# A two-layer hybrid decoder step on eight cores: the order of the token mixing, the first norm's sums, the last group of the output projection and the last block

## What is computed

```python
def trunk_layer(h, ...):                       # two layers, then a final rmsnorm
    z = rmsnorm(h, norm_mix) @ w_in            # 2048 -> 4352: 34 tiles of 128 columns
    # u_a 512, glu_a 768, glu_b 768, sc_b 768, sc_c 768, sc_h 768
    y_a = pool_mixer(u_a)                      # causal means over 2, 4, 8, 16 rows, 128x128 map
    g = glu_a * sigmoid(glu_b)
    cb = layernorm(causal_dwconv31(g) + b)     # width 31
    y_b = silu(cb) @ conf_pw + conf_pw_b
    y_c = sc_b * causal_dwconv3(sc_c * sc_h)   # width 3
    h = h + concat([y_a, y_b, y_c]) @ w_out
    up = rmsnorm(h, norm_ffn) @ w_up
    upc = causal_dwconv3(up)
    h = h + (silu(upc[..., :D_FF]) * upc[..., D_FF:]) @ w_down
    gate = sigmoid(rmsnorm(h, norm_ple) @ ple_gate)
    return h + (p_i @ ple_proj) * gate, <last rows of each convolution's input>
```

## Time and profile before

| | |
|---|---|
| median of 3 runs | 3181.56 us (3180.45 to 3588.96) |
| profiled execution | 3180.19 us |
| its longest span (core 1) | 3178.6 us |
| spans of the other cores | 3168.2 to 3176.3 us |
| TensorE busy, core 1 | 3053.5 us (96%) |
| VectorE | 1717.0 us (54%) |
| ScalarE | 875.0 us (28%) |
| GpSimd | 503.0 us (16%) |

### The profile page before, as it was taken

One profiled execution on the slowest core, in us unless ns is written; L12 is line 12 of the kernel. 1 busy time (PEld: TensorE's weight loads), 2 busy tenths in 40 slices (PEclk: granted clock), 3 DMA queues, 4 the chain that ended last, 5 costly groups with the idle time before them and its releaser, 6 DMA issues.

```text
span 3178.6 us, 58865 instructions; the slowest of 8 cores (3168.2 to 3178.6 us)
## 1 busy us (share of the span) xinstructions
PE 3053.5 (96%) x21015; PEld 1976.6 (62%) x21015; DVE 1717.0 (54%) x3475; ACT 875.0 (28%) x1743; POOL 503.0 (16%) x732
## 2 busy tenths in 40 slices
PE   4899999999999999999999799999999999999995
PEld 1455666666666666666666466666666666666674
DVE  2455425655555555656544633375555555565665
ACT  2214012312131213315551321232212121331565
POOL 4100032010000000015320001311010000001532
PEclk8778999999999999999999999999999999999998
DMA  6543473463544344444346335546444445344444
GB/s 165 113 89 53 70 118 60 80 99 67 85 71 81 70 76 72 81 75 74 61 84 133 58 66 103 78 81 105 74 79 79 79 70 87 69 85 76 74 68 108
DMA packets 126205, 263.28 MB, mean 83 GB/s; under 512 B 36320, under 2 KB 68576, under 8 KB 125920
## 3 DMA queue, kind: packets, MB, share of 16 engines
q0 software_dynamic: 74112, 213.48, 41.0%
q1 hardware_dynamic: 43744, 35.20, 4.5%
q10 hardware_dynamic: 8064, 10.84, 1.4%
HBM read 449.11 MB, written 15.97 MB: 146 GB/s over the span
## 4 chain that ended last, share of the span: by engine, by line
PE 89%; DVE 4%; DMA 2%; issue 1%; ACT 1%; POOL 1%; SPq 1%; ACTq 0%; DVEq 0%; POOLq 0%
PE ps L130 89%; DVE xa L130 2%; DVE U L130 2%; DMA h<-xT 1%; POOL U L130 1%; SPq L130 1%; ACT U L130 1%; DMA U<-hf 0%; DVE h L130 0%; ACT L130 0%; DVE xb L130 0%; ACT rstd L130 0%; ACTq L130 0%; DMA xa<-U 0%; DMA U<-hc 0%
## 5 line engine op out<-in xcount | busy, mean ns | idle before, releaser
L130 PE MATMUL ps<-xa,wb 128*128 128x364 bf16 (+7 forms) x9504 | 1483.4, 319 | 41.5 <-DVE xa L130 19.0
L130 PE MATMUL ps<-xb,wb 128*128 128x366 bf16 (+8 forms) x9760 | 1437.9, 309 | 12.5 <-DVE U L130 9.9
L130 PEld LDWEIGHTS ps<-xa,wb 128*128 128x128 bf16 x9504 | 935.3, 99 | 579.4 <-issue 64.0
L130 PEld LDWEIGHTS ps<-xb,wb 128*128 128x128 bf16 x9760 | 944.3, 98 | 493.8 <-issue 19.0
L130 DVE SCALAR_TENSOR_TENSOR U<-ps,cstt,U 128x348 f32<-128x348 f32 (+3 forms) x1056 | 607.2, 577 | 429.1 <-ACT U L130 372.7
L130 ACT ACTIVATE U<-ps,cstt 128x364 f32<-128x364 f32 (+2 forms) x528 | 290.3, 553 | 1165.6 <-PE ps L130 1105.4
L130 DVE TENSOR_TENSOR h<-ps,h 128x364 f32<-128x364 f32 (+4 forms) x672 | 348.4, 523 | 413.6 <-PE ps L130 412.7
L130 POOL TENSOR_TENSOR U<-U 128x364 f32<-128x364 f32 (+6 forms) x311 | 261.3, 845 | 354.1 <-ACT U L130 347.3
L130 ACT ACTIVATE U<-h 128x344 bf16<-128x344 f32 (+11 forms) x352 | 169.1, 483 | 448.5 <-DVE h L130 394.5
L130 ACT ACTIVATE U<-U 128x364 f32<-128x364 f32 (+4 forms) x418 | 200.5, 480 | 254.5 <-DVE U L130 193.2
L130 POOL DMA_DIRECT2D wb<-w_up x176 | 93.7, 532 | 1051.5 <-PE ps L130 1051.5
(11 more groups left out here) (64 smaller groups left out, 829.5 us busy)
## 6 DMA issues: line engine op xcount, KB each, us to landing
wb<-w_up POOLq DMA_DIRECT2D x176, 512.0 KB, 6.4
wb<-w_in POOLq DMA_DIRECT2D x68, 512.0 KB, 7.0
wb<-w_down POOLq DMA_DIRECT2D x64, 448.0 KB, 6.6
wb<-w_out POOLq DMA_DIRECT2D x32, 512.0 KB, 9.9
wb<-w_down POOLq DMA_DIRECT2D x32, 512.0 KB, 5.4
wb<-ple_gate POOLq DMA_DIRECT2D x32, 512.0 KB, 5.1
h<-xT SPq DMA_DIRECT2D x8, 728.0 KB, 33.3
h<-xT SPq DMA_DIRECT2D x4, 752.0 KB, 14.9
```

The costliest lines, as they stand in the source:

```text
L130: ins = getattr(e, name)(*a, **kw)
```

## The change

1. First norm: ScalarE's 16 squares of a block stay in SBUF (`sq0`), and 16 products by ones sum them; GpSimd adds nothing. `first_norm(b + 1)` now follows `first_rstd(b)`, since all blocks share `sq0`. The weight loads 4 and 5 wait for block 2's input instead of block 1's, and the constants are loaded behind the whole input.
2. Mixing: `sc_triple(0)` stands ahead of `conf_conv(5)`; mean, variance and output of the layer norm are cut into blocks and put behind the blocks of triples 1 and 2; triple 3 follows, then `conf_out`, then the pooling with triples 4 and 5 between its parts. A triple multiplies both h and c by the root (three operations instead of two with its square). `phys` says where in C_t each concatenated tile lies; tile 10 lies in U_t. w_out reads the pooling tiles last, in the first tile as single products. The sample history of the convolution has one buffer instead of two.
3. The last group of w_out has six tiles (`WTAIL`), and `tick` issues the ones product three jobs later.
4. End: three blocks, all pieces on VectorE.

```diff
-                while pend and pend[0][0] <= st["tick"] - 2:
+                while pend and pend[0][0] <= st["tick"] - 3:
...
             def first_norm(b):
                 lo, hi = b0(b)
                 for k in range(KC):
-                    stats0.add(k, b)
+                    S.op("act", (lambda e: e.activation(out=sq0[k][0][:, 0:hi - lo], in_=h1(k, lo, hi), func=AF.Square)), reads=of(hB[k], b), writes=[sq0[k][1]])
...
+            def first_rstd(b):
+                lo, hi = b0(b)
+                slot = bank()
+                mm(slot, hi - lo, KC, (lambda k: ones_t[:]), (lambda k: sq0[k][0][:, 0:hi - lo]), [onesB] + [o for _, o in sq0])
+                rstd_from(slot, of(rsB, b), lo, hi)
...
-                        if first and b < 2:
-                            first_norm(b + 1)
                         slots = [[xjob(wbuf, wv[:, 0], lo, hi, b) for wbuf, wv in ws[j]] for j in js]
                         if b == 2:
                             ring.done(2 * len(js))
                         if first:
-                            go0.pop(0)()
+                            first_rstd(b)
+                            if b < 2:
+                                first_norm(b + 1)
...
-                        S.op("dve", (lambda e: e.tensor_tensor(out=V[:, 0:n + 2], in0=ps_t[:, sc_, 0:n + 2], in1=hv[:, 0:n + 2], op=ALU.mult)),
-                             reads=[psB[sc_], hvB], writes=[VB])
+                        S.op("dve", (lambda e: e.tensor_tensor(out=V[:, 0:n + 2], in0=ps_t[:, sc_, 0:n + 2], in1=rstd_t[:, lo - 2:hi], op=ALU.mult)), reads=[psB[sc_]] + rs, writes=[VB])
+                        S.op("dve", (lambda e: e.tensor_tensor(out=V[:, 0:n + 2], in0=V[:, 0:n + 2], in1=hv_[:, 0:n + 2], op=ALU.mult)), reads=[hvB], writes=[VB])
...
+                        if b in mids:
+                            mids[b]()
...
-                pool_proj(3)
-                conf_dgen(5)
+                sc_triple(0, {0: lambda: conf_dgen(5)})
                 conf_conv(5)
...
+                sc_triple(1, {b: (lambda b=b: ln_mean(b)) for b in range(3)})
+
+                def var_out(b):
+                    if b == 0:
+                        ln_var()
+                    ln_out(b)
+                sc_triple(2, {b: (lambda b=b: var_out(b)) for b in range(3)})
+                sc_triple(3)
+                conf_out()
...
+                pool_proj(3)
                 pool_sums(3)
                 pool_hist(1)
+                sc_triple(4)
                 pool_proj(2)
-                ln_mean()
                 pool_sums(2)
                 pool_hist(0)
+                pool_mm(3)
                 pool_proj(1)
                 pool_sums(1)
                 pool_proj(0)
                 pool_sums(0)
...
-                sc_triple(0)
-                for g in (3, 2, 1, 0):
+                sc_triple(5)
+                for g in (2, 1, 0):
                     pool_mm(g)
-                conf_out()
-                for j in range(1, 6):
-                    sc_triple(j)
...
-                for ms in [[m] for m in range(KC - TAIL)] + [list(range(KC - TAIL, KC))]:
+                for ms in [[m] for m in range(KC - WTAIL)] + [list(range(KC - WTAIL, KC))]:
...
-                eb = Blocks(z0 + 32, (CUT1, CUT2, CUT3, W)) if last else fb
+                eb = fb
...
-                            eng = "pool" if b == eb.n - 1 and k == 12 else "dve"
```

More of the change, by code:

```diff
@@ L371, in go @@
                         slot = bank()
[L372 to L375, removed]
+                        S.op("pe", (lambda e: e.matmul(ps_t[:, slot, 0:n], lhsT=onesf_t[:], rhs=sa[:, 0:n], start=True, stop=False)), reads=[onesB, saB], writes=[psB[slot]])
+                        mm(slot, n, 1, (lambda k: ones_t[:]), (lambda k: sq[:, 0:n]), [onesB, sqb], first=False)
                         rstd_from(slot, of(rsB, b, self.blk.n), lo, hi)
                         self.after(b)
[L378 to L381, removed]
+                    pend.append((st["tick"], go))
             def rstd_from(slot, rb, lo, hi):
@@ L568, in ln_sum, with ln_mean @@
                     return slot, lo, hi, hi - lo
[L570 to L576, removed]
+                def ln_mean(b):
+                    slot, lo, hi, n = ln_sum(b)
+                    for j in JO:
+                        S.op("dve", (lambda e: e.scalar_tensor_tensor(out=CB_v[:, j, lo:hi], in0=ps_t[:, slot, 0:n], scalar=-1.0 / 768, in1=CB_v[:, j, lo:hi],
+                                                                      op0=ALU.mult, op1=ALU.add)), reads=[psB[slot]], writes=[CBB[j][b]])
+                        S.op("act", (lambda e: e.activation(out=sil_v[:, j, lo:hi], in_=CB_v[:, j, lo:hi], func=AF.Square)), reads=[CBB[j][b]], writes=[silB[j][b]])
                 def ln_var():
@@ L686, in after_first @@
                     conf_hist(0)
-                    conf_hist(1)
+                    shs, shsB = late["shs"]
+                    s4 = shs.rearrange("p (j k b) -> p j k b", j=6, k=2)
+                    S.dma("sp", (lambda e: e.dma_start(out=shs.rearrange("p (j c) -> p j c", j=6), in_=hs_in[l])), "s_hs", writes=[shsB])
                     S.dma("pool", (lambda e, l=l: e.dma_start(out=wpl_v, in_=w_pool[l * 512:(l + 1) * 512, :].rearrange("(g c) d -> c g d", c=128))),
@@ L737, in program @@
-                S.op("dve", (lambda e: e.tensor_tensor(out=shc[0].rearrange("p (j b) -> p j b", j=6), in0=s4[:, :, 0, :], in1=s4[:, :, 1, :], op=ALU.add)), reads=[shs[1]], writes=[shc[1]])
-                sc_triple(0)
-                for g in (3, 2, 1, 0):
+                sc_triple(5)
+                for g in (2, 1, 0):
                     pool_mm(g)
-                conf_out()
-                for j in range(1, 6):
-                    sc_triple(j)
                 S.dma("sp", (lambda e: e.dma_start(out=ns_out[l], in_=ns_t[:])), "s_ns", reads=[nsB])
-                cats = catB
+                order = list(range(4, KC)) + list(range(4))
@@ new lines, in wjob, with fn @@
+                def wjob(wbuf, wv, lo, hi, b, split):
+                    slot = bank()
+                    groups = [order[0:11]] + [[k] for k in order[11:]] if split else [order]
+                    for ks in groups:
+                        def fn(e):
+                            for k in ks:
+                                e.matmul(ps_t[:, slot, 0:hi - lo], lhsT=wv[:, k, :], rhs=catv(k, lo, hi), start=(k == order[0]), stop=(k == order[-1]))
+                        S.op("pe", fn, reads=[wbuf] + [catB[k][b] for k in ks], writes=[psB[slot]])
+                    tick()
+                    return slot
```

134 lines of the change are left out of this document (67 added, 67 removed).

## The result

The changed kernel takes 3073.51, 3076.33 and 3076.73 us where the kernel before took 3180.45 and 3181.56: a ratio of 0.9668 (95% interval 0.964 to 0.9696), 106 us less. The forecast was 3103 with a range of 3064 to 3140; what came is rival (a), 3073.

A forecast was written before the change was run, and what follows sets the result against it. TensorE, busy 96% of the span, bounds the kernel, so only its waits and clock losses can be won: -26 - 7 - 5 - 27 - 12 = -77 gives 3103 us with the low clock, -107 or 3073 without; range 3064 to 3140.

The forecast's parts named there:

- rival (a): Whole kernel: no core at clock 0.80, waits go and nothing replaces them; 3073 us, 3064 to 3088; chance 0.28.
- first norm: Start: without GpSimd adds, the second weight pair's products begin at 74 instead of 100.43 us; -26 us.
- layer 0's mixing: Layer 0, convolutions to projection: waits go but the 0.80 clock stays as long; -7 us, or -37 without it.
- layer 1's mixing: Layer 1, same new order: waits for replicas and VectorE go; -27 us, bounds -28 and -14.
- group and tick: Projection's last group of six tiles: VectorE gets more time for norm products; -5 us, bounds 0 and -7.
- plain end: After block 1's last tile: 38 us instead of 50.3, last output issued after about 31; -12, bounds -16 and -4.
- bound of -29: Start: the first norm's gain without the dip to 1.2 GHz while TensorE follows the scalings.
- the -4 of the plain end: End of the kernel: the smallest gain allowed for the plain end, whose term was -12 us.
- VectorE's cover: Mixing: VectorE's triple and layer norm work, 6.8 us a block, fits beside TensorE's at 80 to 95%.
- rival (b): Mixing: VectorE takes TensorE's place, half the waits return; 3120 to 3138 us; 0.21 with (d) and longer low clock.
- Rival (c): Whole kernel slower: low clock holds while TensorE has no long pause; 3450 us if held to 1640; chance 0.06.
- Rival (d): Start shortens less, block 2's input or next weight tiles late; ten of 26 us lost, 3113; within rival (b)'s 0.21.

The follow-up runs named there:

- the one execution that bears on it: Changed kernel with weight tiles three and four released earlier and the last block's squares 13 and 14 summed by TensorE; 3092.33 us, cores 4 and 5 at mean clock 0.986.
- both candidates: Changed kernel with weight tiles three and four released by the input's second quarter, last block's squares 13 and 14 summed by TensorE; 3065.4 to 3066.86 us, ratio 0.9647.

## Why the prediction was right and wrong

| step | forecast | runs |
|---|---|---|
| first norm | -26 | 26 to 28 |
| layer 0's mixing | -7 (-37 without low clock) | 31.6 |
| layer 1's mixing | -27 | 28.8 |
| group and tick | -5 | 2.5, unresolved |
| plain end | -12 | 16 |
| sum | -77 (-107) | 105 to 107; 101 to 105 with 56 or 57 for both mixings, of 106 |

The step that failed is the -7 for layer 0's mixing in the sum: -37 less 30 us of a clock at 0.80, with which the forecast takes it that a core of the changed kernel stands at 0.80 as long again. None did in the three executions. All their mean clocks are between 0.991 and 0.995, the profiled one has 1.00 from 120 to 300 us on every core, and the mixing gave 31.6 us.
The condition itself, "If the clock stands at 0.80 as long again, the gain is -7", is not what the runs speak against: the one execution that bears on it, 3092.33 beside 3065.38 us, lost 27. What had no ground was to take it as the case to forecast, from one execution of the kernel before in which two of eight cores had it. It comes and goes with the execution: of 38 executions of that kernel beside these runs four have cores with a mean clock of 0.970 to 0.972, and the others, at 0.978 to 0.983, take 3173 to 3186 us.
The other part is that the time of the kernel before hardly holds the low clock (4 to 13 us), since it fills what are waits on the other cores. The earlier trace rows already had core 3 without it only 2.7 us behind core 1 in time. So the gain of layer 0 was to be read from core 3, which loses 28.5 us from 140 to 280 us and 20 - 19.77 x 0.83 = 3.6 behind it. That is 32.1, where 31.6 came:

```profile
280.00:300.00 20.00, 19.77 (x108) 11.26 (x109) 3.02 (x12) 14.32 (x29) 1.06 (x2) 0.83 0.30 49
```

My point against rival (a), that 3180.45 and 3181.56 lie above core 3's time, weighed 3 us. That is less than chips differ by: without low clock the kernel before takes 3179 to 3186 us on one of them and 3173 to 3178 on three others.
That -107 without low clock is so close to 106 is partly errors that cancel: layer 0's mixing gave 31.6 instead of 37 and group and tick 2.5 instead of 5, the end 4 us more and layer 1 nearly 2. As forecast, the first two convolutions keep their waits (core 6):

```profile
85.21 6.58 PE L131 MATMUL ps<-xb,U 128*32 128x346 bf16 x96 [3.15 <-DMA xb<-U]
...
98.04 3.77 PE L131 MATMUL ps<-xb,U 128*32 128x346 bf16 x96 [1.22 <-DVE U L131]
```

First norm: right in size and by its chain. Predicted 42.1, 44.6, 62 and 74; the trace has 42.00, 44.55, 61.55 and 71.87. The 1.6 us for a dip in the clock were not needed; without them the sum said 72.4. (The bound of -29 should have been 100.43 - 72.4 = 28, and the -4 of the plain end follows from nothing: 50.3 - 40 is 10.)
Layer 1's mixing: right. No wait of TensorE over 0.43 us (core 6) between the fifth convolution and the projection.
VectorE's cover: right. Its busiest 20 us hold 16.61 us in layer 0 (280 to 300, 83%) and 17.04 in layer 1 (1740 to 1760, 85%), where I had 80 to 95%, and TensorE is busy for all of both; over 140 to 280 VectorE's share is 58%. None of rival (b)'s waits came.
Plain end: the mechanism was right (last output issued 29.9 us after block 1's end, predicted 31), the size off by the landing: I took "the outputs of block 1 are still queued" and 38; it was 34.4. What made the old pieces slow was the run of 728 bytes, which the rule of 512 bytes had made me weigh as queueing.
Rival (c), slower: it did not come, and the mechanism that it rests on is not what ends a low clock. The kernel with both candidates has one profile of an execution that the times leave out (3222.09 us). There cores 6 and 7 have 0.81 until 1000 us, and it ends while TensorE is busy without a gap. The lines are core 6's:

```profile
980.00:1000.00 20.00, 20.00 (x110) 11.82 (x109) 10.28 (x22) 4.89 (x11) 1.16 (x3) 0.81 0.40 62
1000.00:1020.00 20.00, 20.00 (x120) 12.29 (x119) 10.37 (x23) 5.80 (x12) 1.59 (x3) 0.88 0.43 73
1020.00:1040.00 20.00, 20.00 (x133) 12.73 (x131) 9.01 (x19) 5.67 (x12) 1.42 (x2) 1.00 0.52 89
```

Rival (d): nothing of it, the start came as summed.

## What to carry to other kernels

Before a loss on one core is priced, look at the same stretch on a core that does not have it: if that core ends at the same time, the loss is cover for something else, and the gain is to be read there. In the kernel before, a clock loss and waits in the same place were worth about the larger of the two, not the sum. Do not make a state that one execution shows the forecast before you know how often it comes. When an output's transfers are the last thing that the kernel does, split it between whole rows: here that cost 1 us, and halving the rows 30.

## What was not expected of the hardware

- Runs of 728 bytes from SBUF to HBM went at 129 to 135 GB/s a core beside 359 for runs of 2.9 KB, with transfers of equal number and size.
- VectorE's single-input scaling (f32 to bf16, 0.32 us alone) passes once per GpSimd add: 1.03 us.
- The clock of 0.80 came on cores 0 and 1 at the same place in two profiles of the kernel before, taken apart from each other; over 120 to 300 us both had 0.80 or 0.81 and cores 2 and 3 of the same die 0.92 or 0.93, with the dips behind their waits. What calls it up is open. In the profile of 3222.09 us the same level, 0.81, holds on cores 6 and 7 from 100 to 1000 us while cores 4 and 5 of their die have 1.00. The first line is core 1 of the second profile, the other core 3.

```profile
120.00:300.00 180.00, 170.14 (x1258) 98.13 (x1256) 97.56 (x198) 52.49 (x100) 9.22 (x17) 0.81 0.46 82
```
```profile
120.00:300.00 180.00, 157.59 (x1322) 96.62 (x1320) 96.55 (x198) 55.36 (x104) 10.10 (x18) 0.93 0.44 85
```
